# Expert weights fetched in rows of 4 KB instead of 8 KB, and the matching order of the activations

## The reference

```
u = rmsnorm(h, norm_ffn_w)                    # 256 x 1024
logits = u @ [group | expert router]          # 4 + 32 columns
each token goes to the 2 best experts of its best group
for each of 32 experts e, for the tokens x that chose it:
    hid = silu(x @ wg[e]) * (x @ wu[e])       # wg, wu: 1024 x 512
    y  += weight * (hid @ wd[e])              # wd: 512 x 1024
```

## Time and profile before

| | us |
|---|---|
| median of three executions | 1630.69 |
| the profiled execution, its own time | 1629.14 |
| its span | 1627.8 |
| TensorE busy | 1412.9 |
| VectorE busy | 835.7 |
| ScalarE busy | 668.6 |

### The profile page before, as it was taken

One profiled execution on the slowest core, in us unless ns is written; L12 is line 12 of the kernel. 1 busy time (PEld: TensorE's weight loads), 2 busy tenths in 40 slices (PEclk: granted clock), 3 DMA queues, 4 the chain that ended last, 5 costly groups with the idle time before them and its releaser, 6 DMA issues.

```text
span 1627.8 us, 26558 instructions
## 1 busy us (share of the span) xinstructions
PE 1412.9 (87%) x11276; PEld 1171.7 (72%) x11276; DVE 835.7 (51%) x1466; ACT 668.6 (41%) x1084; POOL 10.6 (1%) x10
## 2 busy tenths in 40 slices
PE   7999999999786667667576589999999998999998
PEld 7999898999652233233232389989999986889997
DVE  6775553656621011111111358866776767567775
ACT  6444454533521011011000477455555555455553
POOL 1000000000000000000000010000000000000000
PEclk9999999999998898998978799989999987999999
DMA  6544444458799999999999354324556442235553
GB/s 227 159 153 155 130 156 130 155 182 264 276 368 420 420 420 419 420 421 421 421 421 420 122 182 130 100 79 134 181 182 207 162 132 88 76 128 192 177 181 129
DMA packets 181902, 372.00 MB, mean 229 GB/s; under 512 B 6912, under 2 KB 149376, under 8 KB 157200
## 3 DMA queue, kind: packets, MB, share of 16 engines
q1 hardware_dynamic: 181776, 370.21, 62.0%
HBM read 369.14 MB, written 1.05 MB: 227 GB/s over the span
## 4 chain that ended last, share of the span: by engine, by line
PE 59%; DMA 27%; DVE 7%; ACT 4%; issue 1%; SPq 1%; DVEq 0%; ACTq 0%
DMA wu<-in_expert_w_down_dram 20%; PE bank L565 16%; PE bank L567 16%; PE bank L566 16%; DMA wu<-in_expert_w_up_dram 4%; PE bank L721 3%; DVE lo L533 2%; ACT hi L522 1%; PE bank L1582 1%; DMA raw<-in_hgrn_w_in_dram 1%; PE bank L855 1%; DMA raw<-in_w_in_dram 1%; PE bank L1544 1%; PE bank L830 1%; PE bank L1515 1%
## 5 line engine op out<-in xcount | busy, mean ns | idle before, releaser
L533 DVE TENSOR_TENSOR lo<-raw,hi 128x1024 fp32r<-128x1024 f32 (+2 forms) x315 | 371.6, 1217 | 205.4 <-ACT hi L522 204.7
L565 PE MATMUL bank<-XH,hi 128*128 128x256 f32 x1416 | 405.8, 287 | 4.4 <-DVE lo L533 1.8
L566 PE MATMUL bank<-XL,hi 128*128 128x256 f32 x1416 | 401.1, 283 | 0.0
L567 PE MATMUL bank<-XH,lo 128*128 128x256 f32 x1416 | 400.9, 283 | 0.0
L522 ACT ACTIVATE hi<-raw 128x1024 fp32r<-128x1024 f32 (+2 forms) x315 | 317.0, 1047 | 61.4 <-PE bank L567 23.0
L565 PEld LDWEIGHTS bank<-XH,hi 128*128 128x128 f32 x1416 | 272.0, 192 | 12.8 <-issue 6.7
L1544 PE MATMUL bank<-wu,xg 128*32 128x256 f32 x2048 | 189.3, 454 | 101.8 <-DMA wu<-in_expert_w_up_dram 77.6
L566 PEld LDWEIGHTS bank<-XL,hi 128*128 128x128 f32 x1416 | 271.9, 192 | 0.8
L567 PEld LDWEIGHTS bank<-XH,lo 128*128 128x128 f32 x1416 | 271.8, 192 | 0.0
L1544 PEld LDWEIGHTS bank<-wu,xg 128*32 128x32 f32 x2048 | 75.9, 124 | 195.5 <-DMA wu<-in_expert_w_up_dram 102.8
L1660 ACT ACTIVATE sg<-bank 64x256 f32<-64x256 f32 x32 | 12.0, 376 | 261.6 <-PE bank L1544 261.6
(11 more groups left out here) (355 smaller groups left out, 2171.4 us busy)
## 6 DMA issues: line engine op xcount, KB each, us to landing
wu<-in_expert_w_gate_dram SPq DMA_DIRECT2D x64, 1024.0 KB, 26.7
wu<-in_expert_w_up_dram SPq DMA_DIRECT2D x64, 1024.0 KB, 27.0
wu<-in_expert_w_down_dram SPq DMA_DIRECT2D x64, 1024.0 KB, 27.0
raw<-in_w_in_dram SPq DMA_DIRECT2D x44, 1024.0 KB, 5.1
raw<-in_ffn_w_up_dram SPq DMA_DIRECT2D x44, 1024.0 KB, 5.1
raw<-in_ffn_w_down_dram SPq DMA_DIRECT2D x22, 1024.0 KB, 5.0
raw<-in_hgrn_w_in_dram SPq DMA_DIRECT2D x16, 1024.0 KB, 5.5
raw<-in_w_branch_ret_dram SPq DMA_DIRECT2D x8, 1024.0 KB, 6.0
```

Source lines behind the costliest of these rows:

```text
L533: dve.tensor_tensor(lo_of(u), v, hi_of(u), ALU.subtract).then_inc(*WL.inc(u))
L565: pe.matmul(dst, first[0], first[1], start=start, stop=False)
L566: pe.matmul(dst, second[0], second[1], start=False, stop=False)
L567: return pe.matmul(dst, third[0], third[1], start=False, stop=stop)
```

## The change

Partition p of a gate or up piece now holds rows 2p and 2p+1 of the first 256 rows of the half, and rows 2p and 2p+1 of its second 256: two pieces of 4 KB, 512 KB apart in memory. Partition p of a down piece holds rows p and 128+p, two pieces of 4 KB, 512 KB apart. The slots, the number and order of transfers, the waits and the matmuls stay. The columns of `uH` and `uL` are read at a step of two elements instead of four; the transposes of `hid` read neighbouring columns instead of every second one. The gains' constant and the branch that is not taken are changed to match.

```diff
-    def in_fours(x):
-        return x.rearrange("t (q p four) -> t q four p", p=P, four=4)
+    def paired(x):
+        return x.rearrange("t (q p two) -> t q two p", p=P, two=2)
     def w_place(n):
-        return wslot[w_slot[n]][:, :]
+        s = wslot[w_slot[n]]
+        return s[:, :].rearrange("p (q x) -> p q x", q=2)
     def w_source(n):
         if j < 2:
-            return (wg, wu)[j][e, 512 * half:512 * half + 512, :].rearrange("(p four) c -> p (four c)", p=P, four=4)
-        return wd[e, 256 * half:256 * half + 256, :].rearrange("(p two) c -> p (two c)", p=P, two=2)
+            return (wg, wu)[j][e, 512 * half:512 * half + 512, :].rearrange("(q p two) c -> p q (two c)", p=P, two=2)
+        return wd[e, 256 * half:256 * half + 256, :].rearrange("(k p) c -> p k c", p=P)
 # act_route
-                act.activation(uH[:, i, :].rearrange("t (q four p) -> t q four p", four=4, p=P), in_fours(u2[:, i, :]), ACT.Copy)
+                act.activation(uH[:, i, :].rearrange("t (q two p) -> t q two p", two=2, p=P), paired(u2[:, i, :]), ACT.Copy)
 # dve_route
-                uh, ul = (x[:, i, :].rearrange("t (q four p) -> t q four p", four=4, p=P) for x in (uH, uL))
-                dve.tensor_tensor(ul, in_fours(u2[:, i, :]), uh, ALU.subtract)
+                uh, ul = (x[:, i, :].rearrange("t (q two p) -> t q two p", two=2, p=P) for x in (uH, uL))
+                dve.tensor_tensor(ul, paired(u2[:, i, :]), uh, ALU.subtract)
 # pe_experts, turn_hid
-                    done = pe.transpose(b.ap[:, 64 * c:64 * c + 64], hid[e % 2][:, :].rearrange("t (p two) -> t two p", two=2)[:, c, :],
-                                        ident[0:64, 0:64])
+                    done = pe.transpose(b.ap[:, 64 * c:64 * c + 64], hid[e % 2][:, c * P:(c + 1) * P], ident[0:64, 0:64])
 # sp_fallback (not reached)
-                    rows = w[e].rearrange("(q p four) c -> p q (four c)", p=P, four=4) if j < 2 else w[e].rearrange("(k p) c -> p k c", p=P)
-                    sp.dma_start(wbuf[j][:, :].rearrange("p (q x) -> p q x", q=2 if j < 2 else 4), rows)
+                    rows = w[e].rearrange("(q p two) c -> p q (two c)", p=P, two=2) if j < 2 else w[e].rearrange("(k p) c -> p k c", p=P)
+                    sp.dma_start(wbuf[j][:, :].rearrange("p (q x) -> p q x", q=4), rows)
 # constants
-             "norm_ffn_x": np.asarray(g["norm_ffn_w"]).reshape(2, P, 4).transpose(1, 0, 2).reshape(P, 8)
+             "norm_ffn_x": np.asarray(g["norm_ffn_w"]).reshape(4, P, 2).transpose(1, 0, 2).reshape(P, 8)
```

More of the change, by code:

```diff
@@ L1417, in act_route @@
                 act.wait_ge(*NORM.act.got(1, "x", 3))
-                act.activation(uH[:, i, :].rearrange("t (q four p) -> t q four p", four=4, p=P), in_fours(u2[:, i, :]), ACT.Copy).then_inc(*R.inc("uH", i))
+                act.activation(uH[:, i, :].rearrange("t (q two p) -> t q two p", two=2, p=P), paired(u2[:, i, :]), ACT.Copy).then_inc(*R.inc("uH", i))
             act.wait_ge(*ROUTE.pe.got("logits"))
@@ L1437, in dve_route @@
                 dve.wait_ge(*ROUTE.act.got("uH", i))
-                uh, ul = (x[:, i, :].rearrange("t (q four p) -> t q four p", four=4, p=P) for x in (uH, uL))
-                dve.tensor_tensor(ul, in_fours(u2[:, i, :]), uh, ALU.subtract).then_inc(*R.inc("uL", i))
+                uh, ul = (x[:, i, :].rearrange("t (q two p) -> t q two p", two=2, p=P) for x in (uH, uL))
+                dve.tensor_tensor(ul, paired(u2[:, i, :]), uh, ALU.subtract).then_inc(*R.inc("uL", i))
             rb = PR("rbias", 0, 36).rearrange("p (a n) -> p a n", a=1).to_broadcast([P, 2, 36])
@@ L1744, in sp_fallback @@
                         sp.wait_ge(*(F.pe.got("gu", e - 1, 3) if j < 2 else F.pe.got("dn", e - 1, 3)))
-                    rows = w[e].rearrange("(q p four) c -> p q (four c)", p=P, four=4) if j < 2 else w[e].rearrange("(k p) c -> p k c", p=P)
-                    sp.dma_start(wbuf[j][:, :].rearrange("p (q x) -> p q x", q=2 if j < 2 else 4), rows).then_inc(*FW[j].inc(e, by=16))
+                    rows = w[e].rearrange("(q p two) c -> p q (two c)", p=P, two=2) if j < 2 else w[e].rearrange("(k p) c -> p k c", p=P)
+                    sp.dma_start(wbuf[j][:, :].rearrange("p (q x) -> p q x", q=4), rows).then_inc(*FW[j].inc(e, by=16))
             sp.wait_ge(*F.dve.got("H", NE - 1, 3))
@@ L2693 @@
     parts = {"norm_mix_w": columns(g["norm_mix_w"]), "norm_ffn_w": columns(g["norm_ffn_w"]),
-             "norm_ffn_x": np.asarray(g["norm_ffn_w"]).reshape(2, P, 4).transpose(1, 0, 2).reshape(P, 8), "norm_mix_2": columns(g["norm_mix_2"]),
+             "norm_ffn_x": np.asarray(g["norm_ffn_w"]).reshape(4, P, 2).transpose(1, 0, 2).reshape(P, 8), "norm_mix_2": columns(g["norm_mix_2"]),
              "norm_ffn_2": columns(g["norm_ffn_2"]), "gk_bias": columns(g["gla_gk_bias"]), "gla_norm": columns(g["gla_norm_w"]),
```

## The result

The kernel after the change takes 1638.23 us (median of five executions, 1637.87 to 1638.71), the kernel before 1629.14 us in the same five rounds. The ratio is 1.0055, with a 95% interval of 1.0042 to 1.0068: 9 us slower. I had forecast 1628.3 us and "the same", with 0.23 for slower; the range reached to 1638.0. The time lies 0.2 us above it, near the rival "each packet costs" (1637.7).

A forecast was written before the change was run, and what follows sets the result against it. Bound by the expert fetch plateau's rate and its start. Plateau 0 and routing -2.4 on the profiled 1629.14 gave 1626.7; from the runs' median, 1630.69 - 2.4 = 1628.3 us, "the same"; range 1625.0 to 1638.0.

The forecast's parts named there:

- each packet costs: Rival: on the expert fetch plateau every added packet costs 6.8 ns; +9.4 - 2.4 = +7.0, 1637.7 us; chance 0.23.
- The plateau: Expert fetch, 173 pieces from piece 15: 4 KB packets run at the rate of 8 KB ones, cost 0.
- The 22 windows: Feed-forward down pieces in the last layers, 4 KB packets: 1.5 us windows, mean 422.5 GB/s, taken as the plateau's new rate.
- The bound: Upper bound on the plateau: 6.8 ns per packet, 54 ns per piece, +9.4 us over 173 pieces.
- three cycles per packet: Skill's fixed cost per packet, on the plateau: two 4 KB packets 1.2% dearer than one of 8 KB, 5 us.
- The routing: `uH` and `uL` at a step of two: L1442 starts 2.4 us earlier, and all of it reaches the end.
- The hole before piece 15: DMA engines stand still before piece 15; the hole shrinks from 3.2 to 0.8 us, so the whole 2.4 us arrive.
- The rest at nothing: SyncE's issues, the queue, the transposes of `hid`, the gains' order and the chain after the branch: taken as 0.
- The landing time: Issue to landing of a piece on the plateau: about 14 us if the queue counts packets, or still 27.
- What is late next: After the change the plateau itself is late next: TensorE still waits for transfers all along it.

The follow-up runs named there:

- e3: Transfers alone, all computation left out: stretches of gate-matrix pieces with different packet sizes and numbers in flight; ran once, 679 us.
- e2: Kernel after the change with the expert rows of 8 KB put back, so the output is not the reference's; 1627.87 us, ratio 0.999.

## Why the prediction was wrong

**The plateau, predicted 0, measured +10.7 us: the step that failed.** I compared the 1.5 us windows in the middle of 4 KB pieces that were alone in flight (mean 422.5 GB/s) with the plateau of 8 KB packets in a full queue (420), and concluded that "an 8 KB packet already pays twice what a 4 KB packet pays". These are two different states, read in two different ways. Like with like, 4 KB is slower than 8 KB in both: in e3 419 against 423 GB/s for pieces alone at fixed places (423 against 432 in the best windows), and 410 against 422 in the stream. The 22 windows also read high: laid at the fixed places of e3 they average 415, which is 158 ns a packet and no longer level with the plateau, and the stream has 4096 x 16/410 = 159.8. So part of the packet's cost was hidden by the state and part by where the windows were laid.

The bound was right in kind: 6.8 ns per packet from bursts of 1 and 4 KB, where the kernel paid 67/8 = 8.4 by its bandwidths and 62/8 = 7.7 by its times. My argument against it, that the line gives 432 GB/s for 8 KB "which the plateau never shows", took for granted that burst and plateau can be set side by side; e3 reads 432 for 8 KB pieces alone in the best windows, and 422 in the stream. What inside the DMA engine takes the 9 ns stays open.

The Trainium skill, "DMA: Bandwidth & Descriptors", gives in "iDMA fabric" a stream of 1 MB transfers with 4 KB rows at 408.7 GB/s; this kernel's plateau and e3 agree (409, 410). I had set it aside in favour of short windows. The three cycles per packet of its section "Why small descriptors are slow (HBM only)" made an estimate of 5 us of it, half of what the stream showed.

**The routing, predicted -2.4, measured -2.0 at L1442 and -1.35 at piece 15.** The costs of the step of two were right (2.18 and 2.36 us for the pairs). 0.4 us are missing at L1442 since the norm ahead of it ran 0.2 to 0.4 us later in this execution. The other 0.65 went to TensorE's clock. The windows of the kernel before, to be set beside those of the kernel after above:

```profile
452.00:453.00 1.00, 1.00 (x7) 1.00 (x6) 0.04 (x1) 0.67 (x2) 0.00 (x0) 0.50 0.94 389
453.00:454.00 1.00, 1.00 (x8) 1.00 (x8) 0.00 (x0) 0.32 (x2) 0.00 (x0) 0.78 0.97 389
```

The gather began 2.0 us earlier, at 448.21 instead of 450.22, but the clock rose only half a microsecond earlier. So 21 of its 24 matmuls ran at 0.5, the lower level of 1.2 GHz, instead of 14, and each of those seven took 0.21 us instead of 0.12, some 0.65 us together. In e2, where all 24 did, even less of the gain reached piece 15. I had treated the chain as a block that moves. The measured time of e2, -1.3 us (-3.1 to -0.3), fits this, but its interval holds the forecast -2.4 as well; it is the timelines that decide.

**The hole before piece 15.** Right: the fifteen pieces ahead were done soon after 455, and the hole shrank from 3.2 to about 1 us; piece 15 found no queue ahead of it.

**The rest at nothing.** Right for the issues, the queue and the transposes: e2 holds all of these but the rows and is no slower. The landing time was neither of my two numbers (19.9, not 14 or 27). What is late next was right: the plateau sets the end in every version.

**The chances.** The rival with the right mechanism had 0.23 and named 1637.7 us; the range cut it off at 1638.0, 0.2 us under the result, since it took 6.8 ns as the most a packet could cost. That the rival came within 0.5 us of the time is partly luck: it was reckoned from 1630.69 us, and the kernel before took 1629.14 in the rounds of the result. As a shift it named +7.0 us, and +9.1 were measured.

## What to carry to other kernels

Where a long stream of transfers sets the time, count its packets: here each cost about 9 ns on its DMA engine, so packets of 16, 8, 4 and 2 KB gave 429, 422, 410 and 388 GB/s. Price such a change by rows in the same state, a stream against a stream, and don't lay a short window by hand where few packets decide what it reads. And when a chain in which TensorE's clock rises is moved, look where it rises afterwards, for it may not move along.

## What was not expected of the hardware

Packets of pieces alone in flight took 159 ns (4 KB) and 309 ns (8 KB), in a stream 164 and 312, and three in flight are already the stream. A second issuing queue changes nothing (422 and 422, 409 and 410, 429 and 429). A step of two elements costs VectorE nothing (1.2 us) and ScalarE 0.1 us; steps of four and of eight cost both the same, 2.0 to 2.1 us instead of 1.05 and 1.2. With twice the packets the time from issue to landing fell from 27.0 to 19.9 us; at 2497 and 2564 ns a piece that is 10.8 and 7.8 pieces, or some 1380 and 1990 packets, so by this reckoning the queue holds neither a fixed number of pieces nor one of packets. Small VectorE instructions took 1.04 and 2.61 us instead of 0.17 while GpSimd worked on `uL`. The first mixer ended up to 2.5 us later in some profiles than in others (`uH` starts between 436.3 and 438.8), with rows of 4, 8 and 16 KB; that is as much as the whole gain of the routing. With one profile of each kernel it is open whether the execution or the kernel makes it.
